# Three or four weight units through three norms, and GpSimd adding their squares

## The reference

```
def rmsnorm(x, w):
    y = xf * lax.rsqrt(jnp.mean(xf * xf, axis=-1, keepdims=True) + RMS_EPS)
    return y * w
...
x = x + (normed output of the part before)
u = rmsnorm(x, g) @ w_in          # layer 2: 53 units of 128 columns, up: 48, even: 23
```

## Time and profile before

| | |
|---|---|
| median of 3 runs | 1827.41 us |
| the profiled execution | 1827.75 us, span 1825.7 us |
| busy share of the span | TensorE 80%, weight load 54%, VectorE 39%, ScalarE 32%, GpSimd 2% |
| chain that ended last | DMA 44%, TensorE 36%, VectorE 15%, ScalarE 2%, issue 1% |

### The profile page before, as it was taken

The page is one execution under the profiler, slowest core; times in us unless marked ns, Lnnn a source line. Parts: engine busy times, 40 slices in busy tenths (PEclk is TensorE's granted clock), DMA queues, the critical chain, the costliest instruction groups (busy, mean ns, idle before and its releaser), DMA issues.

```text
span 1825.7 us, 25122 instructions
## 1 busy us (share of the span) xinstructions
PE 1455.1 (80%) x10456; PEld 985.8 (54%) x10456; DVE 707.2 (39%) x1257; ACT 588.5 (32%) x1011; POOL 35.6 (2%) x40
## 2 busy tenths in 40 slices
PE   6999995556656566656656567999999999999998
PEld 4788831111111111112111113998998999999997
DVE  4566600000000000000000000997996998478764
ACT  6444410000000000000000001677476776565654
POOL 0000200000000000000000000000000000000201
PEclk9999897888787886787887877999999999999999
DMA  9566799999999999999999999657453755555330
GB/s 399 221 249 248 308 396 428 429 429 429 428 430 427 429 429 428 430 427 429 429 428 429 428 429 428 235 184 208 159 182 137 273 204 187 185 174 173 139 139 24
DMA packets 53266, 573.55 MB, mean 314 GB/s; under 512 B 4928, under 2 KB 15424, under 8 KB 16576
## 3 DMA queue, kind: packets, MB, share of 16 engines
q1 hardware_dynamic: 47440, 563.10, 76.0%
q10 hardware_dynamic: 5744, 9.28, 1.5%
HBM read 568.04 MB, written 4.33 MB: 314 GB/s over the span
## 4 chain that ended last, share of the span: by engine, by line
DMA 44%; PE 36%; DVE 15%; ACT 2%; issue 1%; SPq 0%; DVEq 0%; ACTq 0%
PE bank L1645 36%; DMA ring<-in_w_gate 14%; DMA ring<-in_w_up 14%; DMA ring<-in_w_down 14%; DVE ring_rounded L2443 6%; DVE work L930 2%; DVE work L748 1%; DMA ring<-in_dense 1%; DVE work L920 1%; DVE work_rounded L2366 1%; DMA work<-decay_rows 1%; ACT work L2126 1%; DVE work L739 1%; ACT weights_high_rounded L2126 1%; DVE work L938 1%
## 5 line engine op out<-in xcount | busy, mean ns | idle before, releaser
L1645 PE MATMUL bank<-ring,work 128*32 128x512 f32 x3008 | 486.3, 781 | 296.4 <-DMA ring<-in_w_up 123.1
L1645 PEld LDWEIGHTS bank<-ring,work 128*32 128x32 f32 x3008 | 94.1, 127 | 652.5 <-DMA ring<-in_w_up 205.8
L2126 ACT ACTIVATE work<-bank 128x512 f32<-128x512 f32 (+3 forms) x156 | 73.9, 489 | 998.9 <-PE bank L1645 666.7
L2443 DVE TENSOR_TENSOR ring_rounded<-ring,weights_high_rounded 128x1024 fp32r<-128x1024 f32 x208 | 252.7, 1220 | 79.7 <-ACT weights_high_rounded L2126 79.7
L2126 ACT ACTIVATE weights_high_rounded<-ring 128x1024 fp32r<-128x1024 f32 x244 | 254.0, 1051 | 42.7 <-PE bank L1645 41.4
L2711 DVE TENSOR_TENSOR work<-work,bank 128x512 f32<-128x512 f32 x16 | 16.5, 1030 | 588.4 <-PE bank L1645 588.4
L1645 PE MATMUL bank<-h_high_rounded,weights_high_rounded 128*128 128x256 f32 x1264 | 184.9, 285 | 3.2 <-ACT h_high_rounded L2126 1.8
L1645 PE MATMUL bank<-h_high_rounded,ring_rounded 128*128 128x256 f32 x1264 | 174.4, 277 | 0.6 <-DVE ring_rounded L2454 0.6
L1645 PE MATMUL bank<-h_normed_rounded,weights_high_rounded 128*128 128x256 f32 x1264 | 173.7, 278 | 0.0
L1645 PEld LDWEIGHTS bank<-h_high_rounded,weights_high_rounded 128*128 128x128 f32 x1264 | 161.2, 188 | 13.7 <-issue 7.2
L1645 PEld LDWEIGHTS bank<-h_high_rounded,ring_rounded 128*128 128x128 f32 x1264 | 158.3, 188 | 1.0 <-DVE ring_rounded L2454 0.8
(11 more groups left out here) (267 smaller groups left out, 1193.1 us busy)
## 6 DMA issues: line engine op xcount, KB each, us to landing
ring<-in_w_gate SPq DMA_DIRECT2D x63, 2048.0 KB, 16.1
ring<-in_w_down SPq DMA_DIRECT2D x63, 2048.0 KB, 16.1
ring<-in_w_up SPq DMA_DIRECT2D x61, 2048.0 KB, 16.4
ring<-in_dense SPq DMA_DIRECT2D x60, 2048.0 KB, 8.3
ring<-in_w_ada SPq DMA_DIRECT2D x12, 2048.0 KB, 13.4
work<-in_w_up SPq DMA_DIRECT2D x3, 1024.0 KB, 14.5
bias_diagonals<-work SPq DMA_DIRECT2D x2, 1536.0 KB, 15.1
ring<-in_dense SPq DMA_DIRECT2D x2, 1024.0 KB, 18.7
```

Source lines behind the costliest of these rows:

```text
L1645: return nc.tensor.matmul(o, lhsT, rhs, start=start, stop=stop)
L2126: return nc.scalar.activation(o, i, f, **kw)
L2443: v.tensor_tensor(as_r(w), w, w_high[:, buffer, :], ALU.subtract).then_inc(s.w_low, 1)
```

## The change

Norms 5, 7 and 9 join those with GpSimd's adds. dense_together becomes dense_through_norm. It takes a lag for each unit: a low-weight matmul of tile k - lag runs beside tile k, and the rest behind the tiles; the column sums are gone, and behind the tiles come the two token sums. At norm 5 three units go through the tiles, with lags 0, 3 and 5, and a fourth whole unit runs between the token sums and spread_roots. At norms 7 and 9 four units go through, two of them with their low weights behind the token sums. The next unit goes into a fifth bank. VectorE copies the spread root to SBUF. At norm 5 GpSimd makes the low weights of units 0 to 2, VectorE only that of unit 3, ahead of the reciprocal. At norm 9 the transposes of the root and ScalarE's copy of it go, and unit 4 runs ahead of the gate projection.

```diff
-ADDED_NORMS = {2: KT - 2, 4: 2, 6: KT - 2, 8: KT - 2, 10: KT - 2, 11: KT - 2}
+ADDED_NORMS = {2: KT - 2, 4: 2, 5: KT - 2, 6: KT - 2, 7: KT - 2, 8: KT - 2, 9: KT - 2, 10: KT - 2, 11: KT - 2}
-TOKEN_NORMS = {2: 7, 4: 4, 6: 6, 8: 6, 11: 6}
+TOKEN_NORMS = {2: 7, 4: 4, 5: 6, 6: 6, 7: 6, 8: 6, 9: 6, 11: 6}
+KEPT_ROWS = (5, 7, 9)
+TOGETHER = 4
...
 # TensorE, layer 2
-            dense_together([... for u in range(2)], *normed, IN_AT["in2"][0], norm=5, low_weights_last=True)
+            first_units = [(d2_block(u), u % UNITS, B[(PU2 + u) % 4], D1_UNITS + u + 1) for u in range(TOGETHER)]
+            dense_through_norm(first_units[:3], (0, 3, 5), *normed, IN_AT["in2"][0], norm=5, behind=first_units[3:])
+            tensor_dense2(pe, dense_unit, TOGETHER, normed, PU2 + TOGETHER, bank=B[5])
...
-            in2(*range(2, 23))
+            in2(*range(TOGETHER + 1, 23))
...
 # TensorE, up (and the same at norm 9, followed by unit 4 in B[5])
+            dense_through_norm([... for u in range(L_UP, L_UP + TOGETHER)], (0, 0, KT, KT), *normed, IN_AT["up"][0], norm=7)
...
 # TensorE, block 3
-            even(2, 3)
-            pe.wait_ge(s.norm_inverted, 10)
-            for t in range(TT):
-                last = nc.tensor.transpose(B[5][:, t * P:(t + 1) * P], RS[:, 1, t * P:(t + 1) * P], ident)
...
 # ScalarE, layer 2
             raw_splits(KT, HH_plain, par("mix_pre"))
+            weight_high(D1_UNITS + 3)
             root(5)
-            weight_high(D1_UNITS + 3)
+            for u in range(2):
+                unit_done(d2_block(u), block_ends(u))
+                weight_high(D1_UNITS + u + AHEAD2)
...
 # VectorE, layer 2
-            weights_low(0, 3)
+            dve.wait_ge(s.w_low, D1_UNITS + 3)
+            weight_low(3)
             norm_invert(5)
...
+                if u == 1:
+                    weight_low(AHEAD2)
                 if u - 1 in CONV_UNITS:
                     tap(u - 1, 1)
-                weight_low(u - 1 + AHEAD2)
+                if u > 1:
+                    weight_low(u - 1 + AHEAD2)
...
 # VectorE, norm_invert
                     dve.wait_ge(s.norm_spread, list(TOKEN_NORMS).index(i) + 1)
+                    if i in KEPT_ROWS:
+                        link(v.tensor_copy(RS[:, i % 2, :], rstd_row(i)))
...
 # GpSimd
-            add_squares(6)
-            add_squares(8)
-            add_squares(10)
+            for unit in range(3):
+                at = D1_UNITS + unit
+                pool.wait_ge(s.w_high, at + 1)
+                w = unit_weights(d2_block(unit), unit % UNITS)
+                nc.gpsimd.tensor_tensor(as_r(w), w, w_high[:, at % HIGHS, :], ALU.subtract).then_inc(s.w_low, 1)
+            for i in (5, 6, 7, 8, 9, 10):
+                add_squares(i)
             add_squares(11)
...
+            def dense_through_norm(units, lags, high, low, base, norm, behind=()):
+
+                def low_weights(unit, k):
+                    block_no, sub, bank, counts = unit
+                    if k == 0:
+                        pe.wait_ge(s.w_low, counts)
+                    ins = mm(bank[:, 0:SEQ], as_r(weights(block_no, sub, k)), high[k], False, k == KT - 1)
+                    if k == KT - 1:
+                        ins.then_inc(s.ring_used if sub == UNITS - 1 else s.dense_mm, 1)
+
+                for k in range(KT + 1):
+                    if k < KT:
+                        pe.wait_ge(s.act_high, base + k + 1)
+                        for _, _, bank, counts in units:
+                            if k == 0:
+                                pe.wait_ge(s.w_high, counts)
+                            mm(bank[:, 0:SEQ], w_high[:, (counts - 1) % HIGHS, k * P:(k + 1) * P], high[k], k == 0, False)
+                        for unit, lag in zip(units, lags):
+                            if 0 <= k - lag < KT - 1:
+                                low_weights(unit, k - lag)
+                    if k:
+                        pe.wait_ge(s.act_low, base + k)
+                        for _, _, bank, counts in units:
+                            mm(bank[:, 0:SEQ], w_high[:, (counts - 1) % HIGHS, (k - 1) * P:k * P], low[k - 1], False, False)
+                ahead = len(units) if behind else sum(lag < KT for lag in lags)
+                for unit, lag in zip(units[:ahead], lags):
+                    for k in range(min(KT - lag, KT - 1), KT):
+                        low_weights(unit, k)
+                added_token_sums(norm)
+                for unit in units[ahead:]:
+                    for k in range(KT):
+                        low_weights(unit, k)
+                for block_no, sub, bank, counts in behind:
+                    dense_unit(block_no, sub, bank, high, low, counts).then_inc(s.ring_used if sub == UNITS - 1 else s.dense_mm, 1)
+                spread_roots(norm, B[5], 0, 0)
```

More of the change, by code:

```diff
@@ L427, in unit_ready, with tensor_dense2 @@
                 dve.wait_ge(s.dense_mm, units_through(unit))
[L429 to L431 removed]
+        def tensor_dense2(pe, dense_unit, unit, act, pu, base=None, first=True, last=True, bank=None):
+            if first and bank is None:
                 pe.wait_ge(s.dense_sb, pu - 3)
[L433 to L434 removed]
+            dense_unit(d2_block(unit), unit % UNITS, B[pu % 4] if bank is None else bank, *act, D1_UNITS + unit + 1, base, first,
+                       last).then_inc(s.ring_used if block_ends(unit) else s.dense_mm, 1)
         def conv_unit(u):
@@ L696, in scalar_block2 @@
             root(7)
+            for u in range(2):
+                unit_done(d2_block(L_UP + u), block_ends(L_UP + u))
+                weight_high(D1_UNITS + L_UP + u + AHEAD2)
             for u in range(2 * FT):
-                unit_done(d2_block(L_UP + u), block_ends(L_UP + u))
+                if u > 1:
+                    unit_done(d2_block(L_UP + u), block_ends(L_UP + u))
                 if u == 40:
@@ L1330, in vector_block3 @@
             scaled(2)
-            dve.wait_ge(s.gl_mm, 2)
+            dve.wait_ge(s.gl_mm, 1)
             for n in range(2):
@@ L1675, in dense_unit @@
                 return ins
-            def dense_together(units, high, low, base, norm, low_weights_last=False):
-                def low_weights(k):
-                    for block_no, sub, bank, counts in units:
-                        if k == 0:
-                            pe.wait_ge(s.w_low, counts)
-                        mm(bank[:, 0:SEQ], as_r(weights(block_no, sub, k)), high[k], False, False)
+            def dense_through_norm(units, lags, high, low, base, norm, behind=()):
[6 more added lines that the diff above has]
+                        ins.then_inc(s.ring_used if sub == UNITS - 1 else s.dense_mm, 1)
                 for k in range(KT + 1):
@@ L1695, in dense_together @@
                     if k:
                         pe.wait_ge(s.act_low, base + k)
-                        for block_no, sub, bank, counts in units:
-                            at = slice((k - 1) * P, k * P)
-                            done = k == KT and not low_weights_last
-                            last = mm(bank[:, 0:SEQ], w_high[:, (counts - 1) % HIGHS, at], low[k - 1], False, done)
-                            if done:
-                                last.then_inc(s.ring_used if sub == UNITS - 1 else s.dense_mm, 1)
@@ L1703, in dense_together @@
-                        column_sum(norm, k - 1)
-                for block_no, sub, bank, counts in units if low_weights_last else ():
-                    pe.wait_ge(s.w_low, counts)
+                        for _, _, bank, counts in units:
[4 more added lines that the diff above has]
+                        low_weights(unit, k)
```

67 lines of the change are left out of this document (31 added, 36 removed).

## The result

| | before | after |
|---|---|---|
| median of the runs timed together | 1827.14 us (4 runs) | 1841.70 us (4 runs, 1840.97 to 1842.38) |
| ratio | | 1.0064, 95% interval 1.0047 to 1.0082 |
| the profiled execution, its span | 1827.75, 1825.7 us | 1842.38, 1840.2 us |

The change costs 14.6 us by the medians (14.5 between the two profiled spans) where 7.6 were predicted, and the time lies above the range. I read the same views in the same order as before.

What follows compares the result with a forecast made beforehand. VectorE was taken to bound norms 5 and 7, its low weight of unit 7 leaving TensorE 0.3 us of room behind norm 9. 5.1 + 1.1 + 1.4 = +7.6 us on 1827.4 gives 1835.0 us; range 1826.5 to 1838.5.

Steps and rivals of the forecast that it cites:

- holds of the low weights: In norm 5's add_normed, GpSimd's low weights 1 and 2 would hold VectorE's two-input operations: 3.7 and 0.3 us.
- holds of the adds: In norm 5's add_normed, GpSimd's six adds of squares would each hold VectorE: 1.0 us together.
- GpSimd can hide 0.39 of a hold behind the first: In add_normed, VectorE's scaled tile (0.39 us, one PSUM input) covers part of each hold; an add costs 0.56 - 0.39.
- Norm 5, handover: Norm 5, last split to product 0: sums, unit 3, spreading, copy; +0.7 us for norm 5 were GpSimd free of side effects.
- Norm 7: Norm 7: product 2 later by +0.5 us, holds in the loop add about 0.6: +1.1 (0.3 to 1.5).
- TensorE is 1.2 to 2 us ahead and has nothing from it: Behind norm 7, TensorE's lead brings no gain, as work taken off it only lengthens a wait.
- A 256-column matmul takes 130/1140 = 0.114 us or a little less: Everywhere: one TensorE pace, used as 0.113 us a matmul, so 2.72 us a unit.
- Norm 9: Norm 9: gate terms +0.97 us behind unit 4, TensorE 0.7 later at unit 7's low weight, holds +0.7: +1.4 (0 to 1.6).
- (a): Rival, all three norms: GpSimd doesn't hold VectorE; +1.9 us, 1829.3 us; chance 0.20.
- (b): Rival, all three norms: TensorE is the bound and the column sums come back; some -6 us, 1821.5 us; chance 0.11.
- (c): Rival: GpSimd is the one kept out, low weights come behind add_normed; +8.6 at norm 5, 1838.5 us in all; chance 0.09.
- (d): Rival: the holds reach only part of add_normed; +4 us, 1831.5 us; chance 0.60 together with the forecast.

Runs made afterwards that it cites:

- n5_only: The kernel before with the change at norm 5 alone; ratio to before 1.0030 (1.0018 to 1.0043).
- n7_only: The kernel before with the change at norm 7 alone; ratio to before 1.0019 (1.0007 to 1.0031).
- n7_delay: Change at norm 7 alone, plus 6 unused float32 calls of ones (1.4 us) behind the root's spreading; ratio to before 1.0036 (1.0019 to 1.0053).
- all_tiny_adds: All three norms changed, but GpSimd's 18 adds of squares take 4 columns in place of 256; ratio to before 1.0057 (1.0042 to 1.0071).
- n7_delay_colsum: Change at norm 7 alone, plus 4 calls of ones and one 256-column float32 matmul behind the spreading; ratio to before 1.0031 (1.0018 to 1.0045).
- n7_colsum: Change at norm 7 alone, plus one unused 256-column float32 matmul with ones behind the root's spreading; ratio to before 1.0021 (1.0009 to 1.0033).
- before_small: The kernel before with eight unused two-column float32 matmuls behind norm 7's last column sum; ratio to before 0.9991 (0.9979 to 1.0004).
- before_spread: The kernel before with four unused 128-column float32 matmuls behind norm 7's last column sum; ratio to before 0.9994 (0.9982 to 1.0006).
- te_tokens: The kernel before with norms 5, 7 and 9 by TensorE's token sums, no GpSimd, two units through the norm; ratio to before 1.0030 (1.0015 to 1.0044).
- te5: The kernel before with norm 5 alone by TensorE's token sums, without GpSimd; 1827.11 us, ratio to before 0.9986 (0.9975 to 0.9997).

## Why the prediction was wrong

- **Norm 5, holds of the low weights: right.** 2.43 and 2.19 us stood where 0.42 did, 3.8 us together (first split at 10.8 instead of 7.0 behind the squares' add); 4.0 were predicted. (The prediction's terms add up to 5.0, where it writes 4.9.) The rule of the Trainium skill ("SBUF — State Buffer", Who interferes with whom) holds here for adds and splits with two inputs in SBUF: 0.95 and 0.75 to 0.81 us where 0.48 and 0.42 stood; the scaled tile, with one input in PSUM, keeps its 0.47.
- **Norm 5, holds of the adds: mis-sized.** 1.0 predicted, 2.3 measured (9.82 less 7.49). The step that failed is "GpSimd can hide 0.39 of a hold behind the first": an add starts when ScalarE's square is done, and that is just ahead of a split (1153.61 and 1153.73), so each costs 0.39 and not 0.17.
- **Norm 5, handover: right**, 0.3 or 0.4 us are left for it and 0.2 were predicted; that VectorE waits there for unit 3 shows as the 2.07 us that the root comes sooner with the spreading first. All of norm 5: 6.5 against 5.1, and it reaches the end (n5_only: 693.1 from the squares' add to the end, 685.8 before).
- **Norm 7: wrong, and it is the step that missed the range.** "TensorE is 1.2 to 2 us ahead and has nothing from it" took a longer wait as free, and "A 256-column matmul takes 130/1140 = 0.114 us or a little less" took one pace for all. The +1.1 at product 2 can't be told, as a fall of the clock in the same place hides it (B and C together: 0.1 longer on average, with kernels 1 to 3 us apart in either group). Behind it U costs 3.0 to 3.7 us (n7_only and after) where I had nothing: in seven of ten traces TensorE runs at 117.8 ns, a unit takes 2.83 us, above VectorE's 2.69 (products of units 2 and 4 in after at 1423.90 and 1429.28), and TensorE becomes the bound (1616 matmuls by 4.5 ns are 7.3 us, less the 3.3 that it waits in the quick pace); in n7_only it ran quickly, waited 3.3 us and lost 2.9 to the clock. Both come to about the same, but an execution can also show neither (n7_delay, 0.3 us) or both (all_tiny_adds, 5.0). What in the change shifts the odds is not settled: neither sort of small float32 matmul does it by itself, and TensorE was kept from VectorE's low weights in two kernels, and was quick in one. So the step that failed and its cost are shown, and the trigger is open.
- **Norm 9: right in mechanism, a little low.** 2.1 to 2.7 against 1.4. Without the adds 0.4 is left, so the holds are 1.7 to 2.3 (0.7 predicted), and 0.4 remains for the handover with unit 4 ahead of the gate (0.7 predicted), which is within what E varies by. TensorE waits for the low weight of unit 7, as said.
- **Rivals.** (a) fell with the first add of 2.43. (b) fell too, but half true: TensorE did become the bound, by running more slowly. (c) fell: GpSimd was not kept out. (d) fell: all eight of GpSimd's operations in the loop held one of VectorE's. The 1.9 us ahead of the change are no part of it: that stretch ends between 1138.6 and 1144.2 over the traces, whatever the kernel.

Sum of what was measured: 6.5 + 3.0 to 3.7 + 2.1 to 2.7 = 11.6 to 12.9 us; the timed ratio gives 8.6 to 15.0 us.

## What to carry to other kernels

GpSimd work with two inputs in SBUF is not free while VectorE runs such operations on the path: count each at its full reading time less only what really lies in front of it, and put it where VectorE reads PSUM or waits. A lead of TensorE over the engine that bounds a stage is not always merely worthless: behind the longer wait at its end the clock can be down, as in n7_only and not in n7_delay. Cut several traces at the same instructions before a difference of 2 us in one is believed; here B alone ran from 227.5 to 232.0 us in the eight kernels with norm 7 as before.

## What was not expected of the hardware

- TensorE has two paces for the same stream at a granted clock of 1.00: 113.3 and 117.8 ns for a 128x128 by 256-column rounded matmul, each held for up to 1600 matmuls. In single traces the slow one began behind small float32 matmuls (n7_delay_colsum), behind a wait (all_tiny_adds, 2.98 us) or behind one start 60 ns late (n7_colsum); that any of these brings it about is not shown, and before_small and before_spread stayed quick behind such matmuls.
- Behind a wait of 3.32 us the clock was down (26 starts 213 ns apart) and behind one of 2.98 too, behind one of 3.00 not; behind one of 1.46, two matmuls after one of 1.16, it was down in before (some 15 such starts at 1374 us) and not in after. The length alone doesn't tell.
- With one such wait filled the fall stood at the next place, at much the same price (B 1.8 us shorter, C 2.6 longer); it stood there too in traces where nothing was filled.
- With two-column float32 sums in place of 256-column ones the clock stood at 0.56 through a whole norm in te_tokens though TensorE was shown busy 22.6 of 23 us; with the same sums at norm 5 (te5, 1145 to 1158 us) and at norm 9 (te_tokens, 1600 to 1625 us) it was 1.00. So the sums alone are not shown to be the cause.
